# Moving the low-part subtractions of 37 weight units from GpSimd to VectorE

## The reference

```python
def first_block(x, ...):
    h = rmsnorm(x, norm1_w)
    rq, rk, rv, rg, mq, mk, mv, ga, gb = split(h @ w_in)
    a = (silu(rg) * retention(rotary(rq), rotary(rk), rv)) @ w_ret_out
    b = moba_attention(rmsnorm(mq), rmsnorm(mk), mv) @ w_moba_out
    x = x + (sigmoid(ga) * a + sigmoid(gb) * b) @ w_o
    h2 = rmsnorm(x, norm2_w)
    return x + (silu(h2 @ w_ffn_gate) * (h2 @ w_ffn_up)) @ w_ffn_down

def second_block(x, p, ...):
    for i in range(2):
        if i == 1:
            k_nope, k_rope, v = shared_kv(x, kv_w_down, kv_norm, kv_w_up, cos, sin)
        x = post_norm(x, 0.5 * swiglu(x, ffn1_w_in[i], ffn1_w_out[i]))
        mix = fox_mixer(x, ...) if i == 0 else mla_mixer(x, ..., k_nope, k_rope, v, cos, sin)
        x = post_norm(x, mix)
        x = post_norm(x, 0.5 * swiglu(x, ffn2_w_in[i], ffn2_w_out[i]))
        gate = sigmoid(x @ ple_w_gate[i] + ple_b_gate[i])
        x = post_norm(x, gate * (p[i] @ ple_w_proj[i]))
    return x
```

## Time and profile before

| | |
|---|---|
| three runs | 1672.57, 1673.18 and 2588.76 us, median 1673.18 us |
| profiled execution | span of 1659.6 us, mean granted clock of PE 0.988 |
| time outside the span, against the median | 13.6 us |
| PE busy | 1580.2 us, 95% |
| DVE, ACT, POOL busy | 904.9, 738.7, 152.4 us |
| subtractions on DVE (L1424) | 215 |
| subtractions on POOL (L449) | 37 |
| HBM read | 272.70 MB, 165 GB/s over the span |

### The profile page before, as it was taken

One profiled execution on the slowest core, in us unless ns is written; L12 is line 12 of the kernel. 1 busy time (PEld: TensorE's weight loads), 2 busy tenths in 40 slices (PEclk: granted clock), 3 DMA queues, 4 the chain that ended last, 5 costly groups with the idle time before them and its releaser, 6 DMA issues.

```text
span 1659.6 us, 24849 instructions
## 1 busy us (share of the span) xinstructions
PE 1580.2 (95%) x10016; PEld 1418.0 (85%) x10016; DVE 904.9 (55%) x1130; ACT 738.7 (45%) x861; POOL 152.4 (9%) x43
## 2 busy tenths in 40 slices
PE   6999999999999999899899998999988989999997
PEld 5877789999899997788799996899988777899995
DVE  4566465555555556324655558755565354665557
ACT  4445445334343345444444346534435553543445
POOL 1010011000100001440100001100023322100001
PEclk9999999999999999899999999999998999999999
DMA  7534345655565554332355554565544223555552
GB/s 276 194 129 151 127 152 185 220 177 187 167 202 194 177 189 145 124 127 77 129 202 193 186 195 160 176 207 178 197 143 153 69 89 113 179 203 179 189 187 91
DMA packets 186863, 274.67 MB, mean 166 GB/s; under 512 B 9952, under 2 KB 137056, under 8 KB 186720
## 3 DMA queue, kind: packets, MB, share of 16 engines
q1 hardware_dynamic: 182848, 261.72, 47.0%
q10 hardware_dynamic: 3952, 12.06, 2.2%
HBM read 272.70 MB, written 1.05 MB: 165 GB/s over the span
## 4 chain that ended last, share of the span: by engine, by line
PE 84%; DVE 10%; ACT 3%; issue 1%; POOL 1%; DMA 1%; ACTq 0%; SPq 0%; DVEq 0%
PE bank L492 19%; PE bank L494 19%; PE bank L493 19%; PE acc L492 6%; PE acc L493 6%; PE acc L494 6%; PE acc L676 2%; DVE w_lo L1424 2%; ACT w_hi L1006 2%; PE acc L488 2%; PE acc L674 1%; PE acc L671 1%; DVE x L1475 1%; PE bank L488 1%; DVE x L1526 1%; DVE tanh L1505 1%
## 5 line engine op out<-in xcount | busy, mean ns | idle before, releaser
L1424 DVE TENSOR_TENSOR w_lo<-w_raw,w_hi 128x2048 fp32r<-128x2048 f32 x215 | 491.1, 2285 | 251.6 <-ACT w_hi L1082 156.5
L492 PE MATMUL bank<-xTh,w_hi 128*128 128x256 f32 x1728 | 490.6, 284 | 0.0
L493 PE MATMUL bank<-xTl,w_hi 128*128 128x256 f32 x1728 | 489.8, 283 | 0.0
L494 PE MATMUL bank<-xTh,w_lo 128*128 128x256 f32 x1728 | 489.7, 283 | 0.0
L1082 ACT ACTIVATE w_hi<-w_raw 128x2048 fp32r<-128x2048 f32 x145 | 276.5, 1907 | 139.9 <-PE bank L494 139.9
L492 PEld LDWEIGHTS bank<-xTh,w_hi 128*128 128x128 f32 x1728 | 332.4, 192 | 2.4 <-issue 0.7
L493 PEld LDWEIGHTS bank<-xTl,w_hi 128*128 128x128 f32 x1728 | 332.4, 192 | 1.7
L494 PEld LDWEIGHTS bank<-xTh,w_lo 128*128 128x128 f32 x1728 | 332.3, 192 | 0.0
L449 POOL TENSOR_TENSOR w_lo<-w_raw,w_hi 128x2048 fp32r<-128x2048 f32 (+2 forms) x37 | 152.1, 4112 | 1474.0 <-ACT w_hi L1006 1474.0
L492 PE MATMUL bank<-w_hi,xTh 128*128 128x512 f32 (+2 forms) x666 | 246.7, 370 | 19.1 <-DVE xTl L1465 12.6
L494 PE MATMUL bank<-w_hi,xTl 128*128 128x512 f32 (+2 forms) x666 | 241.6, 363 | 0.0
(11 more groups left out here) (183 smaller groups left out, 1583.0 us busy)
## 6 DMA issues: line engine op xcount, KB each, us to landing
w_raw<-in_ffn_w_in SPq DMA_DIRECT2D x176, 512.0 KB, 4.4
w_raw<-in_ffn_w_out SPq DMA_DIRECT2D x88, 512.0 KB, 4.2
w_raw<-in_w_in SPq DMA_DIRECT2D x52, 512.0 KB, 4.5
w_raw<-in_fox_w_in SPq DMA_DIRECT2D x24, 512.0 KB, 4.5
w_raw<-in_w_ffn_gate SPq DMA_DIRECT2D x22, 512.0 KB, 4.5
w_raw<-in_w_ffn_up SPq DMA_DIRECT2D x22, 512.0 KB, 4.5
w_raw<-in_w_ffn_down SPq DMA_DIRECT2D x22, 512.0 KB, 4.0
w_raw<-in_ple_w_gate SPq DMA_DIRECT2D x16, 512.0 KB, 4.5
```

Of the source, the lines that this page charges most:

```text
L492: pe.matmul(out, ah, bh, start=first, stop=False)
L493: pe.matmul(out, ah, bl, start=False, stop=False)
L494: return pe.matmul(out, al, bh, start=False, stop=last)
L1424: nc.vector.tensor_tensor(w_lo[slot][:, 0:cols], w_raw[slot][:, 0:cols], w_hi[slot][:, 0:cols].bitcast(F32), ALU.subtract)\
```

## The change

All 37 units go to DVE. `POOL_STAGES` and `pool_units` are gone, and POOL's program has only its two constants. `split_to` subtracts every unit. The places in DVE's program at which it is called stay, which makes the 37 subtractions appear wherever a call passes such a unit. In FoX and MLA, where there were few calls, calls are added at the steps at which ACT rounds the units. Lines behind the first hunks move up by 7 to 14: L1424 becomes L1410.

```diff
-POOL_STAGES = ("kv_down0", "kv_up", "fox_q1", "fox_k1", "fox_q2", "fox_k2", "fox_v5", "fox_q3", "fox_k3", "uq",
-               "mla_oa0", "mla_oa1")
...
-    pool_units = {u for u, unit in enumerate(units) if unit[0] in POOL_STAGES}
-    pool_units |= {unit_at[f"ffn{f}"][0] + 1 for f in range(5)}
-    pool_units |= {unit_at[stage][i] for stage, i in (("rq0", 1), ("rg0", 1), ("moba_out1", 0), ("fox_v4", 1),
-                                                      ("ple_g00", 1), ("ple_g10", 1))}
...
             pool.memset(eps[:, 1:2], RMS_EPS).then_inc(eps_set, 1)
-            for u, unit in enumerate(units):
-                if u in pool_units:
-                    cols, slot = unit[1] * unit[2] or UNIT, u % RING
-                    pool.wait_ge(w_hi_done, u + 1)
-                    pool.tensor_tensor(w_lo[slot][:, 0:cols], w_raw[slot][:, 0:cols],
-                                       w_hi[slot][:, 0:cols].bitcast(F32), ALU.subtract).then_inc(w_lo_done[slot], 1)
...
                 while split[0] < min(n, N_UNITS):
                     u = split[0]
-                    if u not in pool_units:
-                        dve.wait_ge(w_hi_done, u + 1)
-                        lo(u % RING, units[u][1] * units[u][2] or UNIT)
+                    dve.wait_ge(w_hi_done, u + 1)
+                    lo(u % RING, units[u][1] * units[u][2] or UNIT)
                     split[0] += 1
...
-                    uo = unit_at["fox_o0"][0]
+                    u5, uo = unit_at["fox_v5"][0], unit_at["fox_o0"][0]
                     attention("fox", FOX_H, lambda h, t: fo[:, t, h * FOX_DH:(h + 1) * FOX_DH], FOX_DH,
-                              {10: [lambda: split_to(uo + 1)], 11: [lambda: split_to(uo + 2)],
+                              {s: [lambda st=st: ahead(st)] for s, (st, _) in FOX_FILL.items()} |
+                              {5: [lambda: split_to(u5 + RING)], 6: [lambda: ahead("fox_v5")],
+                               10: [lambda: split_to(uo + 1)], 11: [lambda: split_to(uo + 2)],
...
-                    ahead("kv_up", 3)
+                    ahead("kv_up", 2)
...
                     rope_q(0)
+                    ahead("uq", 0)
+                    ahead("kv_up", 3)
                     rope_q(1)
+                    ahead("uq", 1)
...
                     for g in range(2, 8):
-                        fill[2 * g - 3].append(lambda g=g: rope_q(g))
+                        fill[2 * g - 3] += [lambda g=g: rope_q(g), lambda g=g: ahead("uq", g)]
+                    fill[13].append(lambda: split_to(unit_at["mla_oa0"][0] + RING))
                     fill[15] += [lambda t=t: add_chunk("mla_oa", 0, t, (2, 3), ALPHA) for t in range(T)]
+                    fill[15].append(lambda: split_to(unit_at["mla_oa0"][1] + RING))
```

## The result

The changed kernel takes 1698.22 us (median of 4 runs, 1696.77 to 1699.46) against 1673.12 us, a ratio of 1.017 with a 95% interval of 1.014 to 1.020: slower, by less than the 2% that were set as the border. The forecast was 1706 us with a range of 1686 to 1722.

A forecast was written before the change was run, and what follows sets the result against it. PE (TensorE), busy 1580.2 of 1659.6 us, was taken as the bound, so new waits are paid in full. Net pauses of +24.3 us (29.1 + 4.1 - 8.9) and +9 for the clock, on 1673.2, gave 1706 us, range 1686 to 1722.

The forecast's parts named there:

- the eight heads: Start of program, ffn0, ffn1, ffn2, ffn4, fox_v4, ple_g00, ple_g10: PE would newly wait for w_lo from DVE.
- A: Stage heads: the subtraction stands behind the second token tile's low parts on DVE, so PE waits; +29.1 us over eight places.
- B: moba_out1, rg0 and two FoX steps: DVE operations PE needs queue behind a waiting subtraction; +4.1 us.
- C: FoX gates, uq, kv_up, MLA steps, kv_down, ffn3: PE's pauses shrink, mostly as POOL stops holding DVE; -8.9 us.
- The 26 subtractions costed at nothing: kv_down, kv_up, uq, mla_oa and FoX q, k, v units: those inside attention fit DVE's idle time, at no cost.
- D: PE's clock halves behind the eight new stage-head pauses: 1.4 us each, 11.2, less 2.4 for shortened pauses; +9 us.
- The sum's base: Start from the 1673.2 us median, taking its 13.6 us over the 1659.6 us profiled span as time around it that stays.
- The faster one: Rival: all 46 us of DVE stretching lie on PE's path and added subtractions fit idle time; 1627 us, chance 0.04.
- the rival in which the clock stays up: PE's clock does not fall at pauses of about 4 us, so only the pauses are paid; 1697 us, chance 0.20.

The follow-up runs named there:

- e1: The changed kernel with the nine stage-head subtractions given back to POOL (GpSimd): 1661.98 us, 0.996 of the kernel before.
- e2: The kernel before with only the nine stage-head subtractions moved to DVE (VectorE): 1711.15 us, 1.027 of the kernel before.
- e3: The changed kernel with each stage-head subtraction one place earlier, ahead of the second token tile's low parts: 1648.88 us, 0.989 of the kernel before.
- e5: The changed kernel plus GpSimd subtractions reading two SBUF operands of a dead buffer, from ffn1 on, awaited by nothing: 1729.14 us, 1.038 of the kernel before.
- e6: As e5, with GpSimd memsets of the same sizes, which only write SBUF, in place of its subtractions: 1696.72 us, 1.019 of the kernel before.
- e4: The changed kernel with 29 throwaway matmuls before the w_lo wait at the heads of ffn0, ffn1, ffn2 and ffn4: 1689.88 us, 1.013 of the kernel before.
- e7: e3 with the moba_out1 and fox_k1 subtractions also moved, behind the operations they held up: 1641.06 us, 0.985 of the kernel before.

## Why the prediction was right, and where it was off

**The bound and the cause: right.** Waits for w_lo are the new cost, at the eight heads that were named. e1 and e2 undo and repeat exactly this part, and e3 removes most of it by order alone.

**A, +29.1 us: the size was right.** PE's first matmul of ffn0 in the kernel before:

```profile
264.45 0.35 PE L492 MATMUL bank<-w_hi,xTh 128*128 128x256 f32 x1 [1.07 <-DVE xTl L1465]
```

and with the change:

```profile
275.55 0.36 PE L479 MATMUL bank<-w_hi,xTh 128*128 128x256 f32 x1 [1.07 <-DVE xTl L1451]
```

From there to the first matmul with the second unit it was 268.18 - 264.45 = 3.73 us and is 283.30 - 275.55 = 7.75: +4.02 against 4.05. Measured in the same way fox_v4, ffn2 and ffn4 lost 2.0, 2.5 and 3.8 us, where I had 2.3, 3.3 and 4.5. The heads' idle time in all is 98.7 - 71.7 = 27.0 us by e1.

**B, +4.1: the place right, a little too dear.** moba_out0 paused 2.47 us on the operation on bank 0, as argued. In rg0 the pause of 2.49 stayed at 2.49 and one of 0.92 came beside it. The FoX steps show next to none of the 0.8 us that I had for two of them: PE's waits for the attention's output (L1616, before L1630) grew from 1.6 to 1.8 us in all.

**C, -8.9: right in kind.** The gate chain gave 2.9 against 3.0, the pause before uq went, and the MLA steps went from 1.55 to 0.31. In kv_up PE's pause before the transposes fell from 4.68 us to 0.25, and 3.82 came back further on at the subtraction, as said. For kv_down and ffn3 together I had -0.4; kv_down's new pause of 2.97 us was not in it, and it ate up what the shorter waits before it (3.37 to 2.15 and 3.36 to 3.04) and in ffn3 (1.36 to none) gave. B and C come to 71.7 - 79.4 = -7.7 by e1, where I had -4.8. The mechanism is shown by e5 and, for a subtraction, e6. The Trainium skill, "SBUF — State Buffer", section "Who interferes with whom", says that a VectorE instruction with two SBUF inputs contends with one of GpSimd that reads SBUF and not with one that only writes it; both runs agree (3.42 us for a subtraction in e5, 2.29 in e6).

**The 26 subtractions costed at nothing: right for those inside attention.** e1 has all of them, and more, on DVE and is 0.4% faster than before. One of them, kv_down's, is a stage head of the kind of A and gave the pause of 2.97 us; e3, which moves it up as well, doesn't have it.

**D, +9: the step that was mis-sized.** I took 1.4 us a pause and 2.4 off for the pauses that C shortens. By the two profiles PE's busy time grew by 18.0 us. Two of the eight stretches are 6.8 us long and not 3.3, and nothing came back elsewhere: by the mean granted clocks (0.988 and 0.978) the time at half clock grew from some 40 to some 75 us, which is about the 34 us of the eight. e4 gives 2 us a pause.

The rows behind D were also those of a single execution. In the kernel before, the clock stayed up behind rg0's pause of 2.49 us. Behind the same pause in the change it fell:

```profile
131.07 0.64 PE L479 MATMUL bank<-w_hi,xTh 128*128 128x512 f32 x1 [2.49 <-DVE w_lo L1410]
```

```profile
131.30:134.70 3.40, 3.40 (x9) 2.63 (x9) 3.09 (x14) 1.79 (x2) 0.00 (x0) 0.50 0.71 225
```

So it did in e1 to e5 and in e7; it stayed up in e6. The other way round, e6 has the pause of 3.77 us at the start of the program and kept the clock behind it. Its stretches behind the two pauses, at the start and in rg0:

```profile
25.50:32.30 6.80, 6.61 (x29) 5.49 (x30) 2.33 (x2) 0.78 (x1) 0.00 (x0) 1.00 0.84 290
127.50:135.00 7.50, 7.46 (x33) 6.19 (x34) 6.99 (x27) 4.04 (x3) 0.00 (x0) 1.00 0.41 140
```

So the length of a pause alone does not tell whether the clock falls behind it, and putting the eight between a row that kept it and rows that lost it had little to stand on. What else decides is open.

**The sum's base: a wrong reading.** I took the 13.6 us between the profiled span and the median as time around the span. It is 1.8 us: the change's profiled execution took 1698.7 us with a span of 1696.9, and a later run of the kernel before 1661.84 with 1660.0. The profiled execution of before was at the quick end of a spread of 1661.8 to 1673.2 us, over which the mean granted clock goes from 0.987 to 0.979. So the missing 12 us were mostly work at half clock that the profile did not have. Counted from that profile, the clock's part of the loss is the 18 us above. Counted from an execution of before at its median (clock 0.983 over 1666.5 us), it is an estimated 9 us: 0.022 x 1696.9 - 0.017 x 1666.5.

By the two profiles the change cost 37.3 us where the sum had 33: the pauses came out 5 us shorter (19.3 against 24.3) and the clock 9 us dearer. The base was 12 us too high. That the sum came within 8 us of the time is in part luck, since these errors went against each other.

**The rivals.** The faster one fails as its condition does: the operations that were held did get their time back (73 us of subtractions added only 25 us to DVE, so 48 came back where I had counted 46), but PE gained only some 8 us of idle time from it by e1. The time came out at that of the rival in which the clock stays up (1697), which is again the work of the wrong base; the clock did not stay up.

## What to carry to other kernels

When work moves onto an engine with a static order, its cost is set by what stands ahead of it there, not by the engine's load: 2.29 us of work gave 4 us pauses at 55% load, and moved one place up, into a wait of that engine, it gave pauses of 1.5 us or less. For a pause of about 4 us of TensorE some 2 us more for the clock behind it was the mean price of four here. A single one can cost nothing and a shorter one can cost it too, so such a price is better taken from several executions. And before a difference between a profiled span and a median is called overhead, compare time and span of the same execution.

## What the runs showed of the hardware

- GpSimd's subtraction of two SBUF operands held VectorE's two-operand SBUF work for microseconds (0.41 us became 2.96 and 4.71), and a memset of GpSimd that ran for 1.97 us during a subtraction of VectorE left it at its 2.29 us.
- The same pause of TensorE at the same place (2.49 us in rg0, 2.47 in e2) was followed by half clock in seven of the nine profiled kernels and by full clock in two; one of 3.77 us at the start of the program was followed by full clock in e6.
- In e5, VectorE and GpSimd held each other: four operations of GpSimd took 11.96 us there, while two pairs at the mean of 2.14 us an operation would take 8.6.
- The same program on the same chip took 1661.8 to 1673.2 us, with the mean granted clock going with it (0.987 to 0.979). Five runs of e7, with the fewest pauses, lie within 1.5 us, but four of the change lie within 2.7, so it is not shown that pauses make the spread.
